# One step of a hybrid encoder layer: norms per token tile, gates loaded six slabs earlier, cache tiles loaded singly, the sample tile fourth of nine

## What is computed

```python
h = x + 0.5 * post1(SwiGLU_1(pre1(x)))                 # D_FF = 2816
z = pre_mix(h) @ w_in                                  # 5376 columns: q, k, v, rwkv, gates
A = diff_attention(...)   # 4 heads, two softmax maps, rotary; samples also read a cache of 1024 keys and values
B = rwkv7(...)            # 8 heads of 64, a state carried from token to token
m = sigmoid(gA) * (A @ w_o_att) + sigmoid(gB) * (B @ w_o_rwkv)
h = h + post_mix(m @ w_out)
y = h + 0.5 * post2(SwiGLU_2(pre2(h)))
```

## Time and profile before

| | us |
|---|---|
| median of 3 runs | 3202.61 (3199.3 to 3205.78) |
| the profiled execution | 3202.13 |
| its span in the trace | 3200.4 |
| PE busy in the span | 3028.9 (95%) |
| PE loading weights | 2683.5 (84%) |
| DVE, ACT, POOL busy | 1735.0, 1265.1, 473.9 |

### The profile page before, as it was taken

One profiled execution on the slowest core, in us unless ns is written; L12 is line 12 of the kernel. 1 busy time (PEld: TensorE's weight loads), 2 busy tenths in 40 slices (PEclk: granted clock), 3 DMA queues, 4 the chain that ended last, 5 costly groups with the idle time before them and its releaser, 6 DMA issues.

```text
span 3200.4 us, 58193 instructions
## 1 busy us (share of the span) xinstructions
PE 3028.9 (95%) x23816; PEld 2683.5 (84%) x23816; DVE 1735.0 (54%) x2957; ACT 1265.1 (40%) x2494; POOL 473.9 (15%) x609
## 2 busy tenths in 40 slices
PE   7999999998999999999989998999999999999997
PEld 7998999887877878878777787878787889999996
DVE  4455544545344446365676646566575665446444
ACT  4434334434333333343434434443343443344332
POOL 0000000003115133150502304040220100000000
PEclk9999999999999999999989999999999999999998
DMA  5445444566447555352554635342433564445443
GB/s 154 126 128 158 152 128 145 181 198 213 140 150 222 171 184 166 110 157 86 191 167 146 185 115 191 106 144 78 134 117 120 195 206 152 126 145 168 125 128 113
DMA packets 499623, 481.74 MB, mean 151 GB/s; under 512 B 28563, under 2 KB 401708, under 8 KB 499342
## 3 DMA queue, kind: packets, MB, share of 16 engines
q1 hardware_dynamic: 472846, 389.16, 39.5%
q0 software_dynamic: 26512, 88.86, 8.7%
HBM read 430.72 MB, written 48.18 MB: 150 GB/s over the span
## 4 chain that ended last, share of the span: by engine, by line
PE 78%; DVE 9%; DMA 4%; issue 4%; ACT 2%; POOL 2%; SPq 0%; DVEq 0%; ACTq 0%; POOLq 0%
PE ps L246 36%; PE ps L256 27%; PE ps L969 4%; DVE wlo L211 2%; DMA att<-in_cache_att_v_dram 1%; PE ps L1657 1%; PE ps L1739 1%; DVE as L1906 1%; PE ps L1723 1%; PE ps L961 1%; DMA gt<-gates_scratch 1%; ACT whi L203 1%; PE ps L1668 1%; PE ps L268 1%; ACT att L1805 1%
## 5 line engine op out<-in xcount | busy, mean ns | idle before, releaser
L211 DVE TENSOR_TENSOR wlo<-raw,whi 128x512 fp32r<-128x512 f32 x1140 | 818.5, 721 | 901.5 <-ACT whi L203 900.0
L203 ACT ACTIVATE whi<-raw 128x512 fp32r<-128x512 f32 x1140 | 712.7, 629 | 684.2 <-PE ps L246 381.1
L246 PE MATMUL ps<-xnhi,whi 128*128 128x384 f32 x2688 | 930.1, 346 | 18.6 <-DVE xnlo L534 6.9
L246 PE MATMUL ps<-xnhi,wlo 128*128 128x384 f32 x2688 | 906.6, 337 | 0.0
L246 PE MATMUL ps<-xnlo,whi 128*128 128x384 f32 x2688 | 906.3, 337 | 0.0
L246 PEld LDWEIGHTS ps<-xnhi,whi 128*128 128x128 f32 x2688 | 510.5, 190 | 45.5 <-issue 15.5
L246 PEld LDWEIGHTS ps<-xnlo,whi 128*128 128x128 f32 x2688 | 510.9, 190 | 2.3 <-issue 1.9
L246 PEld LDWEIGHTS ps<-xnhi,wlo 128*128 128x128 f32 x2688 | 510.3, 190 | 0.0
L256 PE MATMUL ps<-whi,hidhi 128*128 128x512 f32 x936 | 379.6, 406 | 6.4 <-DVE xnlo L534 4.4
L256 PE MATMUL ps<-whi,hidlo 128*128 128x512 f32 x936 | 367.6, 393 | 0.0
L256 PE MATMUL ps<-wlo,hidhi 128*128 128x512 f32 x936 | 367.5, 393 | 0.0
(11 more groups left out here) (295 smaller groups left out, 3236.2 us busy)
## 6 DMA issues: line engine op xcount, KB each, us to landing
raw<-in_ffn_w_in_dram SPq DMA_DIRECT2D x528, 256.0 KB, 2.9
raw<-in_ffn_w_out_dram SPq DMA_DIRECT2D x264, 256.0 KB, 2.8
raw<-in_w_in_dram SPq DMA_DIRECT2D x252, 256.0 KB, 3.0
xt<-h_scratch SPq DMA_DIRECT2D x36, 512.0 KB, 6.0
att<-in_cache_att_k_dram POOLq DMA_DIRECT2D x32, 512.0 KB, 5.8
att<-in_cache_att_v_dram POOLq DMA_DIRECT2D x32, 512.0 KB, 4.5
rw<-zr_scratch POOLq DMA_DIRECT2D x51, 256.0 KB, 6.8
raw<-in_w_out_dram SPq DMA_DIRECT2D x48, 256.0 KB, 3.0
```

What stands on the lines that cost most here:

```text
L203: act.activation(B["whi"][:, slot], B["raw"][:, slot], ACT.Copy).then_inc(E["whi"], 1)
L211: dve.tensor_tensor(B["wlo"][:, slot], B["raw"][:, slot], B["whi"][:, slot].bitcast(F32), ALU.subtract).then_inc(E["wlo"], 1)
L246: ins = pe.matmul(ps[:, bank, 0:BT], B["w" + wt][:, n % RING, i * P:(i + 1) * P], x(xt, i), start=first and i == 0 and (wt, xt) == passes[ ...
```

## The change

- `TILE_OF` puts the sample tile fourth, so it leads block 1; block 0 is prompt tiles 0 to 2. Rwkv's sample pass and the sample attention move with it. As built, attention has 68 steps in slabs 354 to 447 (1.37 slabs a step), 187 in 449 to 689 (1.28), 92 in 692 to 822 (1.41).
- Z has three steps in place of one; cache tiles are loaded singly (256 KB) into a ring of six with a load per K step, and V is done in three steps of three tiles. T is one step per half of the keys and costs 1.5 in the timetable.
- A post norm has 15 places from 6 slabs before the stage's end: gain first, squares per half tile (the left halves while the right ones are still computed) into a buffer of their own, POOL's three operations per tile, DVE scale for one tile a slab, then add for one tile a slab, stores one by one. The factor 0.5 of the F norms is put into the 1/rms. A pre norm has 8 places, tile by tile.
- Gate pieces 0 and 1 are loaded 6 and 5 slabs before OP begins; the others where they were.
- At the start x is loaded first, then three gains and the identity; the other 15 constants are loaded from POOL's queue, and the scalar is made at slabs 20 to 28. ACT and DVE convert three weight slabs before the first `xnhi` and `xnlo`, and PE's first matmuls of a stage wait for one column group of `xnlo` at a time, where it was four at once.
- The table of negative sines is gone; DVE multiplies by -1 in the same instruction.

```diff
-TILE_OF = [8, 0, 1, 2, 3, 4, 5, 6, 7]
+TILE_OF = [0, 1, 2, 8, 3, 4, 5, 6, 7]
...
 class Banks:
-        self.free = deque((b, None, 0) for b in ids)
-        self.at = {}
+        self.free = deque((b, "xlo", b + 1) for b in ids)
+        self.at = {("x", 0, kk): kk for kk in range(KT)}
...
         for i in range(4):
+            if entered is not None:
+                pe.wait_ge(E["xlo"], entered + i + 1)
...
-POST_STEPS, PRE_STEPS = 7, 5
+POST_STEPS, PRE_STEPS, POST_LEAD = 15, 8, 6
...
-            act.activation(B["gB"][:, :], src, ACT.Square, accum_out=sums[:, tl:tl + 1]).then_inc(E["squared"], 1)
+        act.activation(B["junk"][:, :], src, ACT.Square, accum_out=sums[:, 30 + 2 * tl + hf:31 + 2 * tl + hf]).then_inc(E["squared"], 1)
...
+            pool.tensor_tensor(r, sums[:, tl, 0:1], sums[:, tl, 1:2], ALU.add).then_inc(E["mean_sq"], 1)
...
+        for step in range(POST_STEPS - POST_LEAD - 2):
+            if last:
+                if step < NT:
+                    scale(step)
+                    add(step)
+            elif step < NT:
+                scale(step)
+            elif step < 2 * NT:
+                add(step - NT)
+            yield
...
-        pool.dma_start(Z["kv"][:, i % 3], src).then_inc(E["z_ld%d" % (i % 3)], 16)
+            src = t["cache_att_k" if what == 0 else "cache_att_v"][b, kt * P:(kt + 1) * P]
+            pool.dma_start(Z["kv"][:, i % KV], src).then_inc(E["z_ld%d" % (i % KV)], 16)
...
+                if kt < KTILES:
+                    load(b * 2 * KTILES + KV + kt)
                 yield "K"
...
-                events[start[STAGES.index(("OP", oi))] + max(u, 2 * u - 1)].append("gates")
+                events[start[STAGES.index(("OP", oi))] + (2 * u - 1 if u > 1 else u - 6)].append("gates")
...
-                norm += [start[k + 1] + i for i in range(POST_STEPS)]
+                norm += [start[k + 1] - POST_LEAD + i for i in range(POST_STEPS)]
```

More of the change, by code:

```diff
@@ L237, in claim, with u_slab @@
         bank, sem, count = bk.take(name)
-        if sem is not None:
-            pe.wait_ge(sem, count)
+        pe.wait_ge(E[sem], count)
         return bank
-    def u_slab(bank, x, first, last):
+    def u_slab(bank, x, first, last, entered=None):
         pe.wait_ge(E["wlo"], n + 1)
         for i in range(4):
+            if entered is not None:
+                pe.wait_ge(E["xlo"], entered + i + 1)
             for wt, xt in passes:
@@ L788, in norm_act, with square @@
     sums = B["small"]
+    squares = 0
+    def square(src, tl, hf):
+        if squares:
+            act.wait_ge(E["squared"], squares)
+        act.activation(B["junk"][:, :], src, ACT.Square, accum_out=sums[:, 30 + 2 * tl + hf:31 + 2 * tl + hf]).then_inc(E["squared"], 1)
     for what, k in norm_sequence():
@@ L805, in norm_act @@
-        for tl in range(NT):
-            if what == "pre":
-                act.wait_ge(E["xin%d" % tl], 16 * (posts + pres))
-                src = B["xt"][:, tl]
-            else:
+            yield
+            for tl in range(NT):
+                if tl == 0 and posts + pres:
+                    act.wait_ge(E["mean_sq"], 3 * (posts + pres))
+                act.wait_ge(E["xin%d" % tl], 16 * (posts + pres + 1))
+                for hf in TWO:
+                    square(B["xt"][:, tl, hf * 512:(hf + 1) * 512], tl, hf)
+                    squares += 1
+                yield
@@ L819, in norm_act @@
+                square(B["yb"][:, tl, hf * 512:(hf + 1) * 512], tl, hf)
+                squares += 1
+                yield
+        posts += 1
+        for _ in range(POST_STEPS - POST_LEAD - 3):
             yield
@@ L977, in rw_pe @@
     for p in range(PAIRS):
-        kd = int(p == 0)
+        kd = int(p == SAMPLE)
         tile = TILE_OF[p]
@@ L1705, in att_pe @@
     for n, (blk, h, tile) in enumerate(UNITS):
+        if n == BEFORE:
+            yield from sample()
         first, last_of_head = head_units(n)
@@ L1929, in att_dve @@
         yield "X"
-        yield "T"
+        for c in chunks_of(tile):
+            yield "T"
         yield "V"
@@ new lines, with late_pe, late_act @@
+LATE_AT = (20, 22, 24, 26, 28)
+LATE_LOADS = 15
+def late_pe(pe, B, E):
+    pe.wait_ge(E["late_in"], 16 * LATE_LOADS)
+    pe.wait_ge(E["xlo"], KT)
+    yield
+    yield
+    yield
+    pe.wait_ge(E["set"], 4)
+    pe.wait_ge(E["lam_s"], 3)
+    pe.matmul(B["ps"][:, 6, 0:1], B["gt"][0:1, 1024:1024 + P], B["gt"][0:1, 517:518], start=True, stop=True).then_inc(E["lam_mm"], 1)
+    yield
+    pe.wait_ge(E["lam_in"], 1)
+    pe.wait_ge(E["mask_in"], 1)
+    yield
+def late_act(act, B, E):
+    act.wait_ge(E["late_in"], 16 * LATE_LOADS)
+    yield
+    act.wait_ge(E["lam_s"], 2)
+    act.activation(B["gt"][0:1, 514:516], B["gt"][0:1, 512:514], ACT.Exp).then_inc(E["lam_e"], 1)
+    yield
+    yield
+    yield
+    act.wait_ge(E["lam_in"], 1)
+    act.wait_ge(E["mask_in"], 1)
+    yield
@@ L2216, in weave @@
     for name in gens:
-        assert name == "late" or next(gens[name], "end") == "end", name
+        assert next(gens[name], "end") == "end", name
 def program(nc, t):
@@ L2251, in _ @@
                     next(norm)
+                weights = weights_dve(dve, B, E)
+                for _ in range(AHEAD):
+                    next(weights)
                 dense = dense_dve(dve, B, E, bk)
                 next(dense)
-                weave({"weights": weights_dve(dve, B, E), "dense": dense, "norm": norm, "rw": rw_dve(dve, B, E), "att": att_dve(dve, B, E), "late": late(dve, E)}, 1, AHEAD)
+                weave({"weights": weights, "dense": dense, "norm": norm, "rw": rw_dve(dve, B, E), "att": att_dve(dve, B, E), "late": late_dve(dve, B, E)}, 1, AHEAD, False, AHEAD)
             @block.gpsimd
             def _(pool):
-                next(init_pool(pool, B, E))
+                pool.wait_ge(E["set"], 4)
                 norm = norm_pool(pool, B, E)
```

845 lines of the change are left out of this document (440 added, 405 removed).

## The result

| | before | changed |
|---|---|---|
| median of 4 runs each, us | 3200.95 (3197.7 to 3205.78) | 3173.87 (3167.87 to 3178.82) |
| ratio, 95% interval | 1 | 0.9913 (0.989 to 0.9936) |
| the profiled execution, us | 3202.13 | 3167.87 |
| its span, us | 3200.4 | 3166.0 |

The change is faster by 27 us, where 74.5 were forecast: the time lies inside the stated range, but the gain is little more than a third of what was promised. The profiled execution of the changed kernel is the fastest of its four, so its stage lengths show 34 us less and the medians 27.

A forecast was written before the change was run, and what follows sets the result against it. PE, busy 95% of the span, was taken as the floor, leaving its idle time and 1.2 GHz stretches to win. Six terms summed to -74.5 us, from 3202.1 to 3128 us; range 3098 to 3175.

The forecast's parts named there:

- its work is the same: Sample tile's rwkv pass moved elsewhere: costed at nothing, as the work does not change.
- Term 1: Kernel start: x loaded first and constants moved to POOL's queue bring the first dense matmul earlier; -8.5 us.
- Term 2: Kernel end: gain early, left halves squared early, DVE scale and add tile by tile; -6 us.
- Term 3: Pre norm: loads leave 8 instead of 5 slabs ahead, tiles handled one by one; -5 us.
- Term 4: Sample cache: earlier single loads remove most of 27.3 us idle, and most of 13.8 us clock loss goes; -33 us.
- Term 5: OP stages: early gate pieces cut DVE's gate waits, some idle time and slow clock; -24 us.
- The second rival: OP stages: bound by DVE's work, not its gate wait, so only OP 2's 5.6 us come; 3146 us, 18%.
- Term 6: Prompt units: T per half of the keys gains 8 us, denser score steps cost some 10; +2 us.
- the packing rival: Score steps one slab apart expose their whole chain, 5.5 us for each of 15 pairs; 3208 us, 4%.
- The rule on batching: Sample cache: the skill's fixed 2.0 us per DMA makes single loads cost 128 us more; sum 3256 us.
- The low bounds of the terms: Whole kernel: all terms at their low bounds together, about 3095 us.

The follow-up runs named there:

- sample first: Changed kernel with the sample tile back at the head of block 0 (tile order, stores per block), all other edits kept: 3143.98 us, ratio 0.9823.
- the shift: rwkv's steps 3 slabs earlier or later: changed kernel 3161.12 and 3187.35 us; sample tile first 3149.32 and 3165.24 us, 1 slab later 3149.08 us.

## Why the prediction was wrong

By its own terms, us of the profiled spans:

| term | forecast | sample fourth | sample first |
|---|---|---|---|
| 1 start, up to IP 0 | -8.5 | -11.5 | -10.8 |
| 2 end, last stage | -6 | -4.8 | -4.8 |
| 3, 4, 6 side stages without OP 0 | -36 | -2.9 | -17.3 |
| 5 OP stages | -24 | -15.2 | -22.2 |
| sum | -74.5 | -34.4 | -55.1 |

**What failed is the line that cost the moved sample tile at nothing, "its work is the same".** The work was the same (POOL's 205 more instructions are 64 cache loads, 15 constants and seven operations more in each of 18 norms), what it meets is not. By the prediction's own rule every queue that a step is moved past counts, and the sample turns were moved past rwkv's loads on POOL. The trace of before holds the row that would have shown the stakes, POOL idle behind the sample tile's store and then free for the first head:

```profile
1346.63 0.54 POOL L2006 DMA_DIRECT2D att<-kT_scratch  x1 [4.97 <-DMA attT_scratch<-att]
```

Nothing of rwkv stands between the two, and PE waited 0.3 us for these loads. In place of nothing the runs show 10 to 29 us, by the shift; at the shift of the changed kernel it is 29 of the 47 us that are missing. The prediction's own sign shows the same: it wanted PE's idle time down from 175 to 115 us and the mean clock up to 0.985. The clock came, 0.984; the idle time (span less PE busy) went from 171.5 to 147.9 us only, and with the sample tile first to 126.2.

**Term 1** was mis-sized by 3 us, 2 of them because x was there at 4.37, not at 6.4 us. **Term 2** was 1 us too high: three tiles took DVE 8.7 us from 3152.10, not 7.2, for POOL released each one late.

**Term 3** holds with the sample tile fourth: 4.9 us of pre-norm waits are 1.4. With the sample tile first they are 4.2, on another releaser, DVE's `xnlo`.

**Term 4** had its mechanism and its idle time right, 27.3 us to 1.4. (Its "together 41" counts the 3 us that were to stay; without them its rows give 38.) Its second part fell, the 8.7 us that the clock was to give back. By the trace's clock records the side stages without OP 0 stood at 1.2 GHz for 85.3 us before, 78.5 changed and 81.9 with the sample tile first, so by (1 - PEclk) x length 3.4 and 1.7 us came back: where the slow stretches of the cache waits went, others came with other waits. And the longest stretch follows no gap but the burst of small matmuls, which the cache edit never touched. Even with the sample tile first, where cache waits fell by 24.1 us, the idle time of these stages fell by 18.3 only: other waits took 6 back, as the term had allowed.

**Term 5** came out near its size with the sample tile first and for a reason that is partly another. The gates account for some 9 us beside the old norm and for none that can be told from noise beside the new, and up to 5.7 us of OP 1 are side work that left the stage, which the prediction had not counted. With the sample tile fourth OP 0 got 10 us more of PE's work and 4.5 us of a key transpose's wait, and kept none of its gain. The profile names no releaser for that wait, but in the kernel the transpose waits for DVE's copy of the turn before (L1964), which ends at 1561.67 us behind a norm piece and OP's products, 0.1 us ahead of PE. The second rival, OP bound by DVE's work, is refuted for OP 1, where DVE's busy time fell by 1.1 us and the stage by 9.7. It is refuted for OP 0 too: with the sample tile first and rwkv three slabs later the stage takes 123.5 us, 6.1 less, with 85.0 us of DVE's work in place of 85.6.

**Term 6**: the 15 pairs of score steps one slab apart cost 7.9 us in ten waits of at most 1.4, less than the 12.4 before; the packing rival was never near. The split of T took its wait down by 10.5 us and gained nothing in the time, where 8 us stood.

**The rule on batching**, which gave 3256, is refuted by the time itself and by the value waits, where it was to show first. The low bounds of the terms together give some 3084 us, not 3095; nothing rests on that.

## What to carry to other kernels

An edit that moves a block of work in a statically woven program is never free because the work is the same: lay the moved block's issues and waits on each queue beside what stands there at the new place. In such a program a shift of three slots is worth as much as a careful edit; before an edit's gain or loss of under half a per cent is explained by its mechanism, shift the neighbour by a slot or two and see how far the time moves. Before a stage is called shorter, count its instructions: work may only have left it. And look at what PE did ahead of each slow stretch before it is laid to a gap.

## What the runs showed of the hardware

**Busy PE at 1.2 GHz.** A run of 256 matmuls of 64x16 and the work around it kept PE busy for 22 of 22 us, and the granted clock fell from 1.00 to 0.50 in the middle of the run and stayed there for 17.1 us; with dense slabs between, the same matmuls ran at 1.00. In the run they start 46 ns apart at 2.4 GHz and 85 at 1.2. The Trainium skill ("TensorE: Matmul & The Clock Gate", Terms) prices slow clock at its time multiplied by 1 - K/N. With a half for K/N that makes 8.6 us of the 17.1, an estimate from the page; the trace roughly agrees, with the 7.9 us estimated above from its rows.

**POOL beside DVE.** Two operations on a 128x1 column in the last norm of the changed kernel, alone and then beside DVE's pass over 128x1024 with two inputs:

```profile
3151.24 0.19 POOL L851 TENSOR_SCALAR small<-small 128x1 f32<-128x1 f32 x1
3151.51 0.55 POOL L853 TENSOR_TENSOR small<-small 128x1 f32<-128x1 f32 x1
...
3152.31 1.12 POOL L851 TENSOR_SCALAR small<-small 128x1 f32<-128x1 f32 x1
...
3153.51 1.60 POOL L853 TENSOR_TENSOR small<-small 128x1 f32<-128x1 f32 x1
```

From the first operation's start to the second's are 0.27 us alone and 1.20 us beside DVE, and 0.55 became 1.60; this is what left DVE idle for 0.44 us between tiles. The Trainium skill ("GPSIMD Engine Reference", 1. Specifications) says that POOL's way to the memory is shared with VectorE and contended by instructions with two inputs there; the trace agrees.
